# Sums of squares taken while the blocks of x become final, three more homes for expert panels, and the last pair's down weights in column halves

## The reference

```python
for l in range(2):                                   # first block
    h = rmsnorm(x, norm_mix[l]) * (1 + sc_m) + sh_m
    x = x + gt_m * hybrid_mixer(h, ...)              # ends with mixed @ w_out
    h = rmsnorm(x, norm_ffn[l]) * (1 + sc_f) + sh_f
    x = x + gt_f * ((silu(h @ w_gate) * (h @ w_up)) @ w_down)
# second block, i = 0 (even: attention and mLSTM, with a context xc) and i = 1 (odd: pooling)
    h = modulate(x, g_norm1[i], ...); y = mixer(h, ...)
    x = x + m[2] * y
    h = modulate(x, g_norm2[i], ...)
    x = x + m[5] * ec_moe(h, w_router, w_gate, w_up, w_down)   # 16 experts, 64 tokens each
return rmsnorm(x, g_final)
# rmsnorm: x * rsqrt(mean(x * x over the 1024 features) + eps) * gain
```

## Time and profile before

| | |
|---|---|
| median of 3 runs | 3375.85 us (3368.49 to 3377.31) |
| profiled execution: time, span | 3371.15 us, 3369.4 us |
| TensorE busy | 3022.6 us, 90% of the span, mean granted clock 0.957 |
| VectorE, ScalarE busy | 1110.9 us (33%), 882.0 us (26%) |
| DMA | 637.27 MB, mean 189 GB/s; in the expert stages 404 to 409 GB/s |

### The profile page before, as it was taken

The page is one execution under the profiler, slowest core; times in us unless marked ns, Lnnn a source line. Parts: engine busy times, 40 slices in busy tenths (PEclk is TensorE's granted clock), DMA queues, the critical chain, the costliest instruction groups (busy, mean ns, idle before and its releaser), DMA issues. The chain is left out here.

```text
span 3369.4 us, 41517 instructions
## 1 busy us (share of the span) xinstructions
PE 3022.6 (90%) x18502; PEld 2030.6 (60%) x18502; DVE 1110.9 (33%) x1572; ACT 882.0 (26%) x1328; POOL 0.2 (0%) x4
## 2 busy tenths in 40 slices
PE   5997889999898798999899988789999975999997
PEld 3765768888676676888677667543434353444432
DVE  3446532232536543224343347420001046000002
ACT  3443232231444224223333531311000032010001
POOL 0000000000000000000000000000000000000000
PEclk8998899999998899999999999889999997999999
DMA  7224313323224322322552051279999932999995
GB/s 264 76 100 151 102 63 100 100 82 105 67 79 159 103 89 68 95 94 94 173 173 76 13 215 46 97 301 409 407 409 409 397 105 100 373 409 408 408 409 237
DMA packets 247394, 637.27 MB, mean 189 GB/s; under 512 B 12848, under 2 KB 110128, under 8 KB 247088
## 3 DMA queue, kind: packets, MB, share of 16 engines
q1 hardware_dynamic: 244128, 627.22, 50.1%
q10 hardware_dynamic: 3088, 7.40, 0.6%
HBM read 632.48 MB, written 2.10 MB: 188 GB/s over the span
## 5 line engine op out<-in xcount | busy, mean ns | idle before, releaser
L611 PE MATMUL ps<-mix_halves,work_halves 128*128 128x512 f32 (+1 forms) x1544 | 621.5, 403 | 39.8 <-DVE h_halves L2120 30.9
L611 PE MATMUL ps<-h_halves,work_halves 128*128 128x512 f32 (+1 forms) x1544 | 608.1, 394 | 4.7 <-ACTq L1494 2.4
L611 PE MATMUL ps<-mix_halves,ring_halves 128*128 128x512 f32 x1448 | 567.5, 392 | 0.0
L2120 DVE TENSOR_TENSOR ring_halves<-ring,work_halves 128x2048 fp32r<-128x2048 f32 (+2 forms) x125 | 252.6, 2021 | 543.8 <-ACT work_halves L1503 448.3
L611 PE MATMUL ps<-ring,work 128*64 128x512 f32 x1680 | 389.5, 594 | 23.7 <-DMA ring<-in_w_exp_gate 18.4
L611 PEld LDWEIGHTS ps<-mix_halves,work_halves 128*128 128x128 f32 (+1 forms) x1544 | 290.7, 188 | 127.0 <-issue 42.4
L611 PEld LDWEIGHTS ps<-h_halves,work_halves 128*128 128x128 f32 (+1 forms) x1544 | 291.4, 189 | 72.7 <-issue 6.4
L611 PEld LDWEIGHTS ps<-mix_halves,ring_halves 128*128 128x128 f32 x1448 | 271.8, 188 | 60.2
L1503 ACT ACTIVATE work_halves<-ring 128x2048 fp32r<-128x2048 f32 x102 | 188.2, 1845 | 425.8 <-PE ps L611 333.3
L611 PEld LDWEIGHTS ps<-ring,work 128*64 128x64 f32 x1680 | 128.0, 137 | 257.7 <-issue 257.4
L2518 DVE SCALAR_TENSOR_TENSOR x<-ps,small,x 128x512 f32<-128x512 f32 x112 | 82.2, 749 | 593.9 <-PE ps L611 592.4
(11 more groups left out here) (377 smaller groups left out, 3314.4 us busy)
## 6 DMA issues: line engine op xcount, KB each, us to landing
ring<-in_w_exp_gate SPq DMA_DIRECT2D x114, 1024.0 KB, 11.2
ring<-in_w_exp_down SPq DMA_DIRECT2D x100, 1024.0 KB, 13.0
ring<-in_w_exp_up SPq DMA_DIRECT2D x96, 1024.0 KB, 14.9
ring<-in_ada_w SPq DMA_DIRECT2D x48, 1024.0 KB, 7.1
ring<-in_w_mod SPq DMA_DIRECT2D x48, 1024.0 KB, 7.5
proj<-in_w_exp_up SPq DMA_DIRECT2D x28, 1024.0 KB, 12.9
proj<-in_w_exp_down SPq DMA_DIRECT2D x28, 1024.0 KB, 16.0
ring<-in_w_in SPq DMA_DIRECT2D x22, 1024.0 KB, 5.3
```

Of the source, the lines that this page charges most:

```text
L611: i = pe.matmul(o, lhsT, rhs, start=start, stop=stop, **kw)
L2120: to("lo", tt(rounded(v), v, rounded(hi), ALU.subtract))
```

## The change

It has four parts.

1. Sums of squares. Each squared block gets a place of its own (`sq_mix`, `sq_proj`, `sq_work` take eight blocks in free buffers). ScalarE squares a block once it is final, and TensorE's sums (`square_sums`) stand in its program as follows. In `project_out`: two after m = 3, one after each of m = 4 to 7, two behind the end. In `swiglu`: four before the last down panel, four behind the end. After pooling and after the last `combine`: all eight. At the start: behind the first modulation, with the squares made before it. The even layer's context keeps its own sums, which now begin when the context has landed. A norm then begins with `root(bank)`. The barriers between norm and experts and the second one before the odd norm go. The next weight panel is split earlier, inside `project_out`, `swiglu` of layer 0 and the start; in the odd layer it is split after the root.
2. The final norm applies its gain on VectorE in the same instruction, and the output goes out in four DMAs of two blocks.
3. Three more homes: `act` (between the buffers of the experts' activations, for pair 0), `gates` (in `work`, for pair 0, free after the threshold `r_thr`) and `tables` (`stage_tables`, for all pairs, free after `r_logits`). The gates of tile 0 are made after the first pair's activations. Three semaphores are shared.
4. The last pair's down panels hold 512 columns of four blocks of rows, instead of 1024 columns of two. So columns 0 to 511 are done after four panels, are stored, and `combine` for m = 0 to 3 stands before the last two panels' products.

```diff
-SPARE = (("y", 0, 0), ("y", 2048, 2), ("y", 4096, 4), ("y", 6144, 6), ("h", 0, 0), ("h", 2048, 0))
+SPARE = (("y", 0, 0), ("y", 2048, 2), ("y", 4096, 4), ("y", 6144, 6), ("act", 8192, 0), ("h", 0, 0), ("h", 2048, 0),
+         ("gates", 5120, 0), ("tables", 0, 7))
...
+                            if e == E - 2 and w == "w_exp_down":
+                                v = a[w][l, e + s, j % 2 * 512:j % 2 * 512 + 512, j // 2 * 512:j // 2 * 512 + 512]
+                                panels.append((v.rearrange("(k p) n -> p k n", p=P), 4, 512))
+                                continue
...
-            def norm(of=sq, bank=4):
-                t = of.shape[2]
-                for k in range(KB):
+            def square_sums(of, bank, blocks=range(KB)):
+                for k in blocks:
                     pe.wait_ge(*due("sq"))
-                    mm(ps[:, bank, 0:t], ones, of[:, k % of.shape[1], :], k == 0, k == KB - 1, "sq_sum")
+                    mm(ps[:, bank, 0:of.shape[2]], ones, of[:, k, :], k == 0, k == KB - 1, "sq_sum")
...
                         block(m, w, range(KB))
+                        square_sums(sq_mix, 6, range(0, 2) if m == 3 else range(m - 2, m - 1) if m > 3 else ())
                     free[0] += 1
+                square_sums(sq_mix, 6, range(6, KB))
...
                         w = halved_panel()
+                        if half and k0 + 4 >= FB:
+                            square_sums(sq_proj, 4, range(0, 4))
...
-                    pair(4, e_actT, "e_down")
+                    if p < 7:
+                        pair(4, e_actT, "e_down")
+                for half in range(2):
+                    for j in range(2):
+                        if half and j:
+                            pe.wait_ge(*due("y_sb"))
+                            for m in range(4):
+                                combine(last_pairs, m, m)
+                        w = [panel(), panel()]
+                        for k in range(4 * j, 4 * j + 4):
+                            for e in range(2):
+                                s = slice(e * 64, e * 64 + 64)
+                                mm(ps[s, 4 + half, :], e_actT[:, k, s], w[e][:, k % 4, :],
+                                   k == 0, k == KB - 1, "e_down" if k == KB - 1 and e else None)
+                        free[0] += 2
                 pe.wait_ge(*due("y_sb"))
                 pe.wait_ge(*due("down_x", unread[0]))
-                for m in range(KB):
+                for m in range(4, KB):
                     combine(last_pairs, m, m)
+                square_sums(sq_work, 0)
...
+            def squares(of, signal=None, blocks=range(KB)):
+                for k in blocks:
+                    if signal:
+                        act.wait_ge(*due(signal))
+                    to("sq", f(of[:, k, :], x[:, k, :], ACT.Square))
+            def root(bank):
+                act.wait_ge(*due("sq_sum", KB))
+                link(f(rstd[:, 1, :], ps[:, bank, :], ACT.Ln, scale=1.0 / D, bias=EPS))
+                to("rstd", f(rstd[:, 0, :], rstd[:, 1, :], ACT.Exp, scale=-0.5))
...
             act.dma_start(stage_tables[:, :], a["pool"]).then_inc(sem["pool_in"], 16)
-            barrier()
+            root(0)
             split_panel()
-            norm(x, h, coef[:, 0, :], mod[:, 1, 0, :], mix)
+            norm(h, coef[:, 0, :], mod[:, 1, 0, :], mix)
...
-            norm(x, h, param("final"), None)
-            act.wait_ge(*due("h", 0))
-            act.dma_start(out.rearrange("(k p) t -> p k t", p=P), h).then_inc(sem["stored"], 16)
-            act.wait_ge(sem["stored"], 16)
+            root(0)
+            for k in range(0, KB, 2):
+                act.wait_ge(*due("xn", 2))
+                act.dma_start(out.rearrange("(k p) t -> p k t", p=P)[:, k:k + 2, :], h[:, k:k + 2, :]).then_inc(sem["stored"], 16)
+            act.wait_ge(sem["stored"], 64)
...
-            norm(x, h)
+            dve.wait_ge(*due("rstd"))
+            for k in range(KB):
+                to("xn", stt(out=h[:, k, :], in0=x[:, k, :], scalar=param("final", k), in1=rstd[:, 0, :],
+                             op0=ALU.mult, op1=ALU.mult))
```

More of the change, by code:

```diff
@@ L361, in build @@
         sq, rstd = two(work, 1024), two(work, 2048)
+        sq_mix, sq_proj, sq_work = (cut(v, at, KB * T, k=KB, t=T) for v, at in ((proj_all, 4096), (proj_all, 0), (work, 0)))
         cos_t, sin_t = work[:, 0:T], work[:, T:2 * T]
@@ L530, in slot @@
                 where, start, _ = SPARE[seat[n] - RING]
-                return cut(proj_all if where == "y" else hflat, start, k * width, k=k, n=width)
+                if where == "act":
+                    whole = proj_all[:, start:start + width]
+                    return bass.AP(tensor=whole.tensor, offset=whole.offset, ap=[whole.ap[0], [2048, k], [1, width]])
+                return cut({"y": proj_all, "h": hflat, "gates": work, "tables": stage_tables}[where], start, k * width, k=k, n=width)
             return cut(ring, seat[n] * PANEL, k * width, k=k, n=width)
@@ L1417, in pooling @@
                 free[0] += 1
+                square_sums(sq_proj, 0)
             def layer(l):
-                norm()
                 due("h", KB)
@@ L1450, in even_layer @@
             def even_layer():
-                norm(e_sq)
-                norm(c_sq, 5)
+                square_sums(c_sq, 5)
                 pe.wait_ge(*due("cond"))
@@ L1531, in gate_out @@
                 split_panel()
+                squares(sq_mix, "y_used", range(0, 4))
+                split_panel()
+                squares(sq_mix, "y_used", range(4, KB))
             def conditions(name):
@@ L1798, in norms_even, with root_of @@
             def norms_even():
-                def root(sums, r, tmp):
+                def root_of(sums, r, tmp):
                     link(f(tmp, sums, ACT.Ln, scale=1.0 / D, bias=EPS))
@@ L1986, in experts @@
                     to("aT_sb", f(e_actT, ps[:, 0:2, :].rearrange("p b (i c) -> p (b i) c", i=4), ACT.Copy))
+                    if p < 7:
+                        act.wait_ge(*due("e_down"))
+                        to("y_sb", f(y_store[:, p, :], ps[:, 4:6, :].rearrange("p b f -> p (b f)"), ACT.Copy))
+                for half in range(2):
                     act.wait_ge(*due("e_down"))
-                    to("y_sb", f(y_store[:, p, :], ps[:, 4:6, :].rearrange("p b f -> p (b f)"), ACT.Copy))
+                    to("y_sb", f(y_store[:, 7, half * 512:half * 512 + 512], ps[:, 4 + half, :], ACT.Copy))
                 act.preload_act_table_set("natural_log_exp_and_others")
+                due("down_x", sum(len(blocks) for _, blocks in combining.values()) + 4)
+                squares(sq_work, "down_x")
             def layer(l):
@@ L1993, in layer @@
                     act.dma_start(positions, a["positions"].partition_broadcast(P)).then_inc(sem["pos_in"], 16)
-                split_panel()
-                norm(x, h, coef[:, 0, :], mod[:, 0, 0, :], mix)
+                root(4)
+                norm(h, coef[:, 0, :], mod[:, 0, 0, :], mix)
                 split_panel()
@@ L2006, in layer @@
                 barrier()
+                root(6)
+                norm(h, coef[:, 1, :], mod[:, 0, 3, :], mix)
                 split_panel()
-                norm(x, h, coef[:, 1, :], mod[:, 0, 3, :], mix)
-                split_panel()
-                swiglu()
+                swiglu(l)
                 barrier()
@@ L2018, in _ @@
             conditions("start")
+            act.wait_ge(sem["x_in"], 16)
+            squares(sq_proj)
             for i in range(2):
@@ L2024, in _, with moe_layer @@
                 layer(l)
-            def moe_layer(w):
+            def moe_layer(w, bank):
                 barrier()
-                norm(x, h, coef[:, 1, :], mod[:, w, 3, :])
-                barrier()
+                root(bank)
+                norm(h, coef[:, 1, :], mod[:, w, 3, :])
                 experts(w)
@@ L2870, in layer @@
             def layer(l):
-                lower_panels()
-                norm(x, h, mix)
+                norm(h, mix)
                 lower_panels()
@@ L2902, in moe_layer @@
                 barrier()
-                norm(x, h)
-                barrier()
+                norm(h)
                 experts(mod[:, w, 5, :], w)
```

85 lines of the change are left out of this document (44 added, 41 removed).

## The result

The kernel after takes 3340.5 us (median of 4 runs, 3337.1 to 3342.4), the kernel before on the same chip 3375.0 (4 runs, 3368.5 to 3377.3): a ratio of 0.990 with a 95% interval of 0.988 to 0.992. Forecast were 3341 us, in a range of 3322 to 3360. The profiled execution took 3342.4 us, its span is 3340.7 instead of 3369.4.

A forecast was written before the change was run, and what follows sets the result against it. TensorE, busy nine tenths of the span, was taken as the bound, with DMA nearly always busy only in expert stages. Terms sum to 32.1 us: 3339 from the profiled execution, 3343.8 from the median; forecast 3341, range 3322 to 3360.

The forecast's parts named there:

- ffn norm, layer 0: From the output projection's last product to layer 0's first ffn product: 11.6 us instead of 16.9, gain 5.3.
- mix norm, layer 1: From the last product before layer 1's mix norm to the first behind it: 11.9 us instead of 18.1, gain 6.2.
- mix norm, layer 0: At the start, squares made while TensorE waits for modulation panels: first product at 53.6 instead of 56.80, gain 3.2.
- even norm: Before the even layer: the context's DMA is issued later, behind the barrier, so a loss of 6.2 us (4.4 to 10).
- first experts' norm: From the last product before the first experts to their logits done: 15.6 us instead of 20.7, gain 5.1.
- last pair and odd norm: From the first experts' last product to the odd layer's first product: 23.6 us instead of 25.9, gain 2.3.
- second experts' norm: From the pooling products to the second experts' logits: end at 2826.1 instead of 2830.86, gain 4.8 us.
- the end: Last product to output landed: 2.4 us gained up to the root, 3.7 behind it with four output DMAs, 6.1 together.
- homes: Three more panels loaded early in each expert stage: 7.7 us of lead, taken at nothing because storage binds at panel 28.
- rival of stalled sums: Sums find no ready square and TensorE waits within the projection; half of five norms' 27 us goes: 3355, chance 0.12.
- The sign: At the even norm: the modulation products start about 18 to 20 us behind T, the last product, instead of 13.7.
- The sign that would have spoken for the homes: An expert stage shorter than now from logits to last product, less 3.6 of moved combines, would show the forecast wrong.

The follow-up runs named there:

- homes_back: The kernel after with its three new homes taken out again, the gates' products staying where the change moved them: 3342.2 us, ratio 0.989.
- ctx_early: The kernel after with layer 1's last squares in `mix` and the even layer's two DMAs issued inside layer 1's down product: 3328.6 us, ratio 0.986.
- h_homes: The kernel after with the two homes in `h` open for pair 1 too, all four gate tiles turned in pair 2: 3331.1 us, ratio 0.985.
- rows_back: The kernel after with the last pair's down weights cut by rows again and all eight combines behind them: 3336.9 us, ratio 0.987.
- best_all: best_mod plus three idle-time products covering TensorE's pauses at the start of the even attention: 3307.5 us, ratio 0.980.
- best_mod: The kernel after with h_homes, ctx_early, the odd layer's panel split before the barrier, and one even modulation vector ahead of the context's sums: 3307.3 us, ratio 0.981.

## Why the prediction was right

Each term against the two profiles, both counted from the last product T, with sums and combines that moved ahead of T added back:

| term | forecast, us | measured, us |
|---|---|---|
| ffn norm, layer 0 | 5.3 | 5.3 (16.9 to 11.6) |
| mix norm, layer 1 | 6.2 | 6.2 (18.1 to 8.3 + 3.6) |
| mix norm, layer 0 | 3.2 | 4.5 (56.80 to 52.28) |
| even norm | -6.2 | -7.5 (26.4 to 30.4 + 3.6) |
| first experts' norm | 5.1 | 5.0 (20.7 to 11.3 + 4.4) |
| last pair and odd norm | 2.3 | 2.1 (25.9 to 20.2 + 3.6) |
| second experts' norm | 4.8 | 5.2 (20.7 to 15.5) |
| the end | 6.1 | 6.9 (32.1 to 21.6 + 3.6) |
| homes | 0 | 0 (homes_back, and the waits of both profiles) |

Layer 1's ffn norm measures the same 5.3, and with it the measured terms sum to 33.0 us; forecast were 32.1. The spans differ by 28.7, since stretches that the change doesn't touch came out 4.3 longer in this pair of profiles, above all between the even norm and the even output projection (7.7 longer; the two layers' mixers 3.1 and 2.5 shorter). The two profiles of the kernel before differ by 7.7 in that same stretch, so a difference of this size is scatter, which the medians mostly even out: they differ by 34.5. My choice of 3341, between the sum from the profiled execution and the one from the median, lies 0.5 us off the measured median. As the profiled execution lay below the median, the sum from the median, 3343.8, had the better ground, and part of the closeness is luck. So is that two terms missed by 1.3 us in opposite directions.

**Norms.** The order of the argument held: what goes is the work of ScalarE and VectorE before and between sums. A sum among products costs its 0.89. The rival of stalled sums had its test in the output blocks, which follow each other every 6.35 us (5.44 and 0.9), without idle time.

**Mix norm of layer 0.** I kept the low clock's 9.17 for its sums; they took 7.97:

```profile
39.78 7.97 PE L623 MATMUL ps<-proj,consts 128*128 128x512 f32 x16
52.28 0.76 PE L623 MATMUL ps<-mix_halves,work_halves 128*128 128x512 f32 x1 [4.53 <-DVE h_halves L2168]
```

With ready squares they follow the modulation products without a pause, where the earlier trace rows have one of 3.25, and the granted clock over them is 0.88 instead of 0.82. Here the term was mis-sized by 1.3.

**Even norm.** The mechanism was as told. It was mis-sized by 1.3: the context's sums took 6.5 us behind a pause of 7.9, where I had allowed 3.6 and half of it again. The sign missed as well: by the prediction's count, which has all eight sums of x behind T, the modulation products start 21.4 us behind T (17.8 with four of the sums ahead of it), not 18 to 20. ctx_early shows both the cause (the issue behind the barrier) and the clock's share (3.69 without the pause).

**Homes.** The pauses came as forecast, 13 and 9 us, and h_homes shows the cause: three more panels ahead of panel 28 are worth nothing, while two homes that are open for panels 28 and 29 took 4.1 and 5.1 us out of TensorE's waits in the two stages. The sign that would have spoken for the homes, a shorter stage, did not show: from the end of the second logits to the last expert product the kernel before takes 506.5 us, and the kernel after 510.0 less the 3.6 of the moved combines, 506.5.

**Last pair.** The parts that I summed for it were right, but the text doesn't say what rows_back shows: cutting those weights into column halves is worth nothing, and the gain of the tail comes from squares that are ready in time (rows_back: 15.2 us from T to the root, 17.4 before).

**Output.** 10.3 us from the root to the end, 10.6 forecast. DMA issues of the kernel after at the end:

```profile
out<-h ACTq DMA_DIRECT2D x4, 512.0 KB, 2.9
```

The four transfers land 2.9 us after their issue (the middle of the four) and overlap. The 2 MB of one take 7.1, so by my estimate from this pair the part that doesn't grow with size is (4 x 2.9 - 7.1) / 3 = 1.5 us, not 2.0. The 2.0 that the Trainium skill gives in DMA: Bandwidth & Descriptors, Anatomy of one DMA, is a fit for DMAs issued from GpSimd, and these are issued from ScalarE. The Trainium skill, DMA: Bandwidth & Descriptors, Rules for kernel authors, advises to coalesce many small transfers and names those under 64 KB as mostly overhead; these have 512 KB. Here the cut gained 4.0 us, as only the last transfer stands behind VectorE's last block.

## What to carry to other kernels

Measure a norm from the last product before it to the first one behind it, and ask which engine fills each microsecond: moving the squares forward pays for other engines' time, not for the sums. More prefetch storage pays only if it is open at the panel where the stream first waits for storage; count the order of seats, then look for the dry stretch in the DMA rows. When a buffer gets a second use, look at which DMA now has to wait for it: here that cost 7.5 us and a free buffer elsewhere gave 8.7 back.

## What the runs showed of the hardware

The granted clock at one place is not the same in two profiles of one kernel: 1.00 and then 0.53 over 11 us, behind the same pauses of 1.2 and 2.3 us. From the even projection to the logits the second took 7.7 us more, some 5 of them at this place. In both profiles of kernels with those pauses covered the clock stayed at 2.4 GHz there, but best_all took as long as best_mod. The Trainium skill, TensorE: Matmul & The Clock Gate, Part 1, says that the monitor behind the clock runs free of the kernel, so that the slow start of one kernel differs from run to run. It tells this of the start; the two profiles of the kernel before show a drop in the middle that comes in one and not in the other, and no run shows why. best_all gave its 5 us back over the next 250 us, part of them at a lower clock (0.90 instead of 1.00 in the stretch shown); why the clock was lower there was not settled.
